# Routing from residual rows in two halves of tokens, gathering unnormalised rows, and a ninth weight slot

## The chip, the cores and the metric

The kernel runs on one core of one Trainium2 chip. The metric is the time of one execution in microseconds (us). The core's engines are TensorE (PE in the rows, its weight loads PEld), VectorE (DVE), ScalarE (ACT), GpSimd (POOL) and SyncE (SP, here the queue that issues nearly all DMAs). SBUF holds 128 partitions; PSUM has eight banks of 128 x 512 float32.

## The reference

One layer on 512 tokens of width 1024, all in float32: a mixer, then a mixture of experts (MoE), then a gated embedding, each added to the residual. What matters here is the second part:

```python
u = rms_norm(h, norm_ffn_g)                 # h * rsqrt(mean(h*h) + eps) * g
group_logits = u @ w_rg + b_rg              # 4 groups: the best one
exp_logits   = u @ w_re + b_re              # 8 experts a group: the best two of that group
gates = p_group * softmax(top_v)
for each expert e, each token that chose it:
    y = (silu(x @ w_gate_e[e]) * (x @ w_up_e[e])) @ w_down_e[e]     # 1024 -> 512 -> 1024
h = h + sum over the two choices of gate * y
```

There are 32 experts with three matrices of 2 MB each, 96 matrices or 201 MB in all. A token's two experts are computed and no others, but every expert's weights are read.

## The kernel before

**Stages.** The mixer is 15 blocks of four tiles: each tile is a product of float32 numbers that were split into a rounded high half (fp32r) and the rest, so a product takes three passes of 128 x 512. The last two blocks are `out`: tile c of them writes half of the residual of token block c % 4 (`residual`, lines 969 to 974), so that the four token blocks of 128 tokens (`h1` in `r1`) are complete one after the other, after tiles 4, 5, 6 and 7.

**Routing.** When a token block's residual is complete, ScalarE takes the sum of squares and the root (`norm`), VectorE multiplies by the root and the gain (`normalise`, line 859) and writes `u2` in an order of columns that lets TensorE read it in contiguous pieces. TensorE transposes `u2` (`transpose_rows`, line 1194), ScalarE copies the transposes to `u2T`, and `logits` makes the 36 logits of three token blocks at once and of the last block alone, transposed, with the router's weights as the stationary operand. `logits_by_token` turns them back and adds the two halves. VectorE then runs a chain of some twenty small operations on all four token blocks (`first_max` and what stands around it, lines 1036 to 1051), TensorE counts places (`before`, `ones`), and VectorE makes `pick`, a matrix of zeros and ones that says which token stands in which of the 64 places of each of two experts. `gather` multiplies the halves of `u2` (`u2_high`, `u2_low`) by `pick`: 8 products of 128 x 512 for each half of the columns. ScalarE copies the rows to `xrow`, TensorE transposes them (`transpose_x`, line 1331) and ScalarE copies the result to `xT`.

**Expert loop.** For each expert: `gate_and_up` (32 matmuls in two column tiles of 64), one half of the `gather` for the next pair of experts, `gather_info` (token numbers and gates, 8 small matmuls), `down` of the expert before (8 matmuls), on odd experts `transpose_x` for the next pair, and two transposes of the hidden rows. A float32 matmul shows as two records, so 32 of them are 64 rows in the trace. VectorE scales the result and GpSimd scatters it to DRAM by an indirect DMA. The order within the loop is written by hand, and is the same on each engine's queue at every run.

**Weights.** The 96 matrices go through the eight 2 MB slots of `ring` in a fixed order (`loads`): gate, up of expert 0 and 1, down of 0, then gate, up of e and down of e - 1. Eight of them are loaded ahead of the loop: two at the end of block 12, two after the first `out` block, four after the last (line 449; the last of these waits for the logits as well, whose transposes lie in slot 7). In the loop SP issues matrix n when matrix n - 8 has been read.

**Tail.** After the loop the two results of each token are read back (`y_back`), added to `h1` (line 1129), normalised, transposed and multiplied by the gate matrix (`ple_gate`), while TensorE also computes the embedding product (`ple`).

Of the kernel before, what the change touches and what calls it, by code (L numbers as in the profile page):

```python
# [15 lines left out]
ALU = mybir.AluOpType  # L16
# [15 lines left out]
SLOT = 4096  # L32
C = 64
# [3 lines left out]
def build(nc, x, p, norm_mix_g, w_in, conv_w, conv_b, w_rg, b_rg, w_ig, b_ig, lru_lambda, w_pool, pool_scale,  # L37
# [17 lines left out]
    assert NE % 4 == 0 and (3 * NE) % SLOTS == 0 and S == 512 and D == 1024  # L55
# [34 lines left out]
    with ctx:  # L90
# [27 lines left out]
        u2 = r2[:, :].rearrange("p (i d) -> p i d", i=TT)  # L118
        merged = r3[:, :].rearrange("p (k t) -> p k t", k=KD)
        u2T = ring[:, 7, :].rearrange("p (k t) -> p k t", k=KD)  # L120
# [46 lines left out]
        lgT = r4[:, 0:S]  # L167
        logit_parts = (slice(0, (TT - 1) * P), slice((TT - 1) * P, S))

# [3 lines left out]
        u2_low = r2_r[:, :].rearrange("p (i d) -> p i d", i=TT)  # L173
        u2_high = r3_r[:, :].rearrange("p (i d) -> p i d", i=TT)
        pick = sb("pick", [P, TT, 2, C], F32R)
# [4 lines left out]
        vecs = sb("vecs", [P, P])  # L180
# [20 lines left out]
        add_halves = sb("add_halves", [P, NL])  # L201
        g4 = sb("g4", [P, 4, TT, NG])
        t4 = sb("t4", [P, 12, TT])
        el = sb("el", [P, TT, NE])
        cand = sb("cand", [P, TT, NE])
# [18 lines left out]
        slot_full = [sem(f"slot_full{s}") for s in range(SLOTS)]  # L224
# [48 lines left out]
        lgT_psum = sem("lgT_psum")  # L273
        lgT_cleared = sem("lgT_cleared")
        lgT_ready = sem("lgT_ready")
        lgT_ready2 = sem("lgT_ready2")
# [9 lines left out]
        u2_high_ready = sem("u2_high_ready")  # L286
        u2_low_ready = sem("u2_low_ready")
# [19 lines left out]
        row_free = sem("row_free")  # L307
        y_in = [[sem(f"y_in{k}_{i}") for i in range(TT)] for k in range(2)]
# [18 lines left out]
        def slots_at(m):  # L327

            return 16 * (m // SLOTS + 1)


# [25 lines left out]
        def split_u2(eng, api, i):  # L357

            eng.wait_ge(u2_high_ready, i + 1)
            eng.wait_ge(ut_psum, 2 * (TT + i) + 2)  # L360
            api.tensor_tensor(u2_low[:, i, :], u2[:, i, :], u2_high[:, i, :], ALU.subtract).then_inc(u2_low_ready, 1)
# [6 lines left out]
        def wslot(n, k):  # L368
            return ring[:, n % SLOTS, :].rearrange("p (k f) -> p k f", k=k)


        T_PLE = 0
        T_PG = T_PLE + 1
        s0 = T_PLE % SLOTS
        wple = ring[:, s0, 0:KP * D].rearrange("p (k n) -> p k n", k=KP)
        p_rows = ring[:, s0, KP * D:KP * D + TT * KP * P].rearrange("p (i n) -> p i n", i=TT)
        pT = ring[:, s0, KP * D + TT * KP * P:KP * D + 2 * TT * KP * P].rearrange("p (k t) -> p k t", k=KP)
        y_back = ring[:, 5:7, :].rearrange("p s (i k d) -> p (s i) k d", i=2, k=2)
        ple = ring[:, 7, :].rearrange("p (i d) -> p i d", i=TT)
        u3 = u2  # L380
        u3T_high = slot_r[0][:, :].rearrange("p (k t) -> p k t", k=KD)
        u3T_low = merged_low
# [7 lines left out]
        def gate_part(kind, h):  # L390
            of = {"whole": ring[:, T_PG + h, :], "low": slot_r[T_PG + h][:, :], "high": slot_r[T_PG + 2 + h][:, :]}[kind]
            return of.rearrange("p (k f) -> p k f", k=KD)
# [5 lines left out]
        def _(sp):  # L398
# [6 lines left out]
            def small_loads():  # L405
# [13 lines left out]
                sp.dma_start(wrt[:, :, 0:NG], w_router_group[0].rearrange("(p k) n -> p k n", p=P)).then_inc(lru_in, 16)  # L419
                sp.dma_start(wrt[:, :, NG:NL], w_router_expert[0].rearrange("(p k) n -> p k n", p=P)).then_inc(lru_in, 16)  # L420
# [18 lines left out]
            def load_expert(n):  # L439

                which, e = loads[n % (3 * NE)]
                dst = ring[:, n % SLOTS, :]
# [8 lines left out]
            for m, n in ((0, FIRST_OUT), (6, FIRST_OUT), (3, FIRST_OUT + 1), (4, FIRST_OUT + 1),  # L451
                         (1, FIRST_OUT + 2), (2, FIRST_OUT + 2), (5, FIRST_OUT + 2), (7, FIRST_OUT + 2)):
                sp.wait_ge(tile_done, 4 * n)
                if m == 7:
                    sp.wait_ge(logits_psum, 1)
# [141 lines left out]
        def _(act):  # L597
# [148 lines left out]
            for i in range(TT - 1):  # L746
                u2_round(i)
# [731 lines left out]
```

## Time and profile before

| | |
|---|---|
| median of 3 runs | 918.71 us (914.36, 918.71, 919.59) |
| profiled execution | 918.7 us, its span 917.0 us |
| mean granted TensorE clock | 0.982 |
| busy: PE, PEld, DVE, ACT, POOL | 875.6, 583.8, 360.8, 260.5, 105.5 us |
| HBM read and written | 247.93 MB and 10.49 MB |

The span has four stretches: the mixer to about 352 us, routing and the first gather to 381 us, the expert loop to 842 us, and the tail to 917 us. A row of the chain of waits gives a start, a length, and what was being waited for or done; a row of the timeline gives start, busy time, engine, line, operation, output and inputs, and at its end the idle time before it with what ended it. The 1.7 us between the span and the time lie outside the instructions.

### The profile page before, as it was taken

The page shows a single profiled execution, that of the slowest core. Times are in us where ns is not written, and L with a number is a line of the kernel's source. Part 1 is how long each engine was busy: PE and PEld are TensorE (multiplying, and loading weights), DVE is VectorE, ACT ScalarE, POOL GpSimd, SP SyncE. Part 2 cuts the span into 40 slices and gives each one's busy share as a digit, 9 for nine tenths or more (in the row PEclk, how much of TensorE's full clock was granted, in tenths as well). Part 3 has the DMA queues.
Part 4 walks back from the last instruction along what each step waited for, and adds up shares of the span by engine and source line. Part 5 has one row for each costly group of instructions (what it writes and reads, how often), then busy time and mean ns, then how long its engine had stood idle before and what let it go on. Part 6 is the DMA issues. An engine that isn't in the chain of part 4 may idle for free.

```text
span 917.0 us, 12501 instructions
## 1 busy us (share of the span) xinstructions
PE 875.6 (95%) x5343; PEld 583.8 (64%) x5343; DVE 360.8 (39%) x544; ACT 260.5 (28%) x371; POOL 105.5 (12%) x82
## 2 busy tenths in 40 slices
PE   4999899999999997799999999999999999999896
PEld 3778687778888885555555555555555555554575
DVE  6599419952751635321121111211112111122865
ACT  7565326633232225110111001110101101011657
POOL 3429470000000001000000000000000000000000
PEclk8999999999999999799999999999999999999998
DMA  9222222211524665399999999999999999998802
GB/s 259 82 93 92 91 92 92 91 46 47 184 92 184 233 249 240 150 403 424 428 427 427 426 429 424 426 427 426 430 425 427 426 427 427 424 427 335 299 1 92
DMA packets 43295, 255.03 MB, mean 278 GB/s; under 512 B 8594, under 2 KB 9686, under 8 KB 30952
## 3 DMA queue, kind: packets, MB, share of 16 engines
q1 hardware_dynamic: 40248, 248.46, 66.8%
q0 software_dynamic: 2560, 4.20, 1.2%
q10 hardware_dynamic: 432, 1.57, 0.4%
q8 instruction: 42, 0.69, 0.3%
q14 instruction: 13, 0.11, 0.0%
HBM read 247.93 MB, written 10.49 MB: 282 GB/s over the span
## 4 chain that ended last, share of the span: by engine, by line
PE 81%; DVE 8%; DMA 6%; ACT 3%; issue 1%; SPq 0%; DVEq 0%; POOLq 0%; ACTq 0%
PE bank L1180 78%; DMA ring<-in_w_down_e_dram 4%; PE bank L1331 2%; DVE ring L922 1%; DVE ring L926 1%; PE bank L1365 1%; PE bank L1194 1%; DVE r L928 1%; DMA ring<-expert_rows 1%; DVE r L859 1%; DMA r<-in_x_dram 1%; DMA expert_rows<-r,row_i 1%; ACT junk L610 0%; DVE ring_rounded L343 0%; ACT ring_rounded L338 0%
## 5 line engine op out<-in xcount | busy, mean ns | idle before, releaser
L1180 PE MATMUL bank<-ring_rounded,ring_rounded 128*128 128x512 f32 x704 | 246.2, 393 | 1.7 <-ACT ring L798 1.7
L1180 PE MATMUL bank<-ring,junk 128*64 128x256 f32 x2048 | 240.5, 391 | 1.1 <-issue 0.6
L1180 PE MATMUL bank<-r_rounded,ring_rounded 128*128 128x512 f32 x704 | 231.8, 400 | 4.8 <-DVE ring_rounded L343 2.8
L1180 PEld LDWEIGHTS bank<-ring,junk 128*64 128x64 f32 x2048 | 141.4, 135 | 88.2 <-issue 4.8
L1180 PEld LDWEIGHTS bank<-r_rounded,ring_rounded 128*128 128x128 f32 x704 | 133.8, 190 | 36.9 <-DVE ring_rounded L343 3.6
L1180 PEld LDWEIGHTS bank<-ring_rounded,ring_rounded 128*128 128x128 f32 x704 | 132.9, 189 | 31.9 <-issue 2.4
L1180 PE MATMUL bank<-ring,hT 128*64 128x512 f32 x512 | 116.6, 597 | 0.7 <-DMA ring<-in_w_down_e_dram 0.7
L1103 DVE TENSOR_TENSOR sig<-sig,bank 128x256 f32<-128x256 f32 x32 | 13.5, 422 | 221.3 <-ACT sig L782 221.3
L782 ACT ACTIVATE sig<-bank 128x256 f32<-128x256 f32 x32 | 12.3, 385 | 297.7 <-PE bank L1180 297.7
L586 POOL DMA_INDIRECT expert_rows<-r,row_i x32 | 31.4, 981 | 448.3 <-DVE r L1085 448.3
L1180 PE MATMUL bank<-r_rounded,pick 128*128 128x512 f32 x272 | 72.9, 412 | 1.6 <-DVE pick L1030 1.6
L1180 PEld LDWEIGHTS bank<-ring,hT 128*64 128x64 f32 x512 | 34.2, 137 | 61.2 <-issue 59.9
L1085 DVE TENSOR_SCALAR r<-bank,gate_c 128x512 f32<-128x512 f32 x32 | 24.0, 751 | 117.3 <-PE bank L1180 117.3
L338 ACT ACTIVATE ring_rounded<-ring 128x2048 fp32r<-128x2048 f32 x28 | 53.6, 1913 | 43.1 <-DMA ring<-in_w_in_dram 18.5
L343 DVE TENSOR_TENSOR ring_rounded<-ring,ring_rounded 128x2048 fp32r<-128x2048 f32 x19 | 43.5, 2288 | 54.6 <-ACT ring_rounded L338 54.6
L1180 PEld LDWEIGHTS bank<-r_rounded,pick 128*128 128x128 f32 x272 | 49.7, 192 | 23.9 <-issue 14.6
L1180 PE MATMUL bank<-ring_rounded,r_rounded 128*128 128x512 f32 x128 | 49.9, 389 | 0.0
L343 POOL TENSOR_TENSOR ring_rounded<-ring,ring_rounded 128x2048 fp32r<-128x2048 f32 x9 | 42.4, 4727 | 63.6 <-ACT ring_rounded L338 63.6
L762 ACT ACTIVATE gain<-bank 128x512 f32<-128x512 f32 x34 | 20.3, 597 | 59.2 <-PE bank L1180 59.2
L766 ACT ACTIVATE junk<-bank 128x512 f32<-128x512 f32 x34 | 18.6, 595 | 58.2 <-PE bank L1331 58.2
L908 DVE SCALAR_TENSOR_TENSOR ring<-bank,prm,ring 128x511 f32<-128x511 f32 (+2 forms) x24 | 17.9, 747 | 37.1 <-ACT ring L646 36.5
L1180 PEld LDWEIGHTS bank<-ring_rounded,r_rounded 128*128 128x128 f32 x128 | 24.0, 188 | 4.9
(186 smaller groups left out, 650.5 us busy)
## 6 DMA issues: line engine op xcount, KB each, us to landing
ring<-in_w_gate_e_dram SPq DMA_DIRECT2D x32, 2048.0 KB
ring<-in_w_up_e_dram SPq DMA_DIRECT2D x32, 2048.0 KB
ring<-in_w_down_e_dram SPq DMA_DIRECT2D x32, 2048.0 KB
ring<-in_w_in_dram SPq DMA_DIRECT2D x18, 1024.0 KB, 7.2
r<-in_x_dram SPq DMA_DIRECT2D x8, 512.0 KB, 8.1
ring<-in_w_up_a_dram SPq DMA_DIRECT2D x4, 1024.0 KB, 6.2
ring<-in_w_out_dram SPq DMA_DIRECT2D x4, 1024.0 KB, 6.3
ring<-in_w_ple_gate_dram SPq DMA_DIRECT2D x4, 1024.0 KB, 14.0
```

The lines of the kernel that those rows point to most:

```text
L338: nc.scalar.activation(high_half(n, h), whole_half(n, h), ACT.Copy).then_inc(high_ready, 1)
L343: api.tensor_tensor(low_half(n, h), whole_half(n, h), high_half(n, h), ALU.subtract).then_inc(low_ready[low_engine[n, h]], 1)
L586: nc.gpsimd.indirect_dma_start(out=y_halves, out_offset=bass.IndirectOffsetOnAxis(ap=row_i[:, e:e + 1], axis=0), in_=yrow[:, e % 4, :], in ...
L762: nc.scalar.activation(xrow[:, h * HALF:(h + 1) * HALF], bank[6 + h][:, :], ACT.Copy).then_inc(xrow_ready, 1)
L766: nc.scalar.activation(xT[:, 4 * h:4 * h + 4, :, :].rearrange("p k e c -> p k (e c)"), bank[6 + h][:, :].rearrange("p (k n) -> p k n", k=4 ...
L782: nc.scalar.activation(sig[:, :], bank[2 + e % 2][:, 0:FE // 2], ACT.Sigmoid).then_inc(sig_ready, 1)
L859: v.scalar_tensor_tensor(out=dst, in0=src, scalar=rstd[:, q:q + 1], in1=view(gain[:, :]), op0=ALU.mult, op1=ALU.mult).then_inc(norm_done, 1)
L908: ins = v.scalar_tensor_tensor(out=y[:, d:S], in0=z[:, 0:S - d], scalar=tap(3 - d, c), in1=y[:, d:S], op0=ALU.mult, op1=ALU.add)
L1085: v.tensor_scalar(yrow[:, e % 4, :], bank[5][:, :], gate_c[:, e:e + 1], None, ALU.mult).then_inc(y_stored, 1)
L1103: v.tensor_tensor(sig[:, :], sig[:, :], gate_up[:, 0:FE // 2], ALU.mult).then_inc(gated, 1)
L1180: return nc.tensor.matmul(*a, **k)
L1331: ins = nc.tensor.transpose(bank[6 + h][:, k * P:(k + 1) * P], xrow[:, (4 * h + k) * P:(4 * h + k + 1) * P], ident[:, :])
```

## The change

**Routing.** No normalised rows are made. TensorE transposes the residual rows themselves (`transpose_h1`, with the stationary operand read at every 8th column), in the middle of the next `out` tile; the gain is multiplied into the router's weights once (`wrt`), and the root into the logits (`rstd` as the scalar of the first routing operation). The logits are made one token block at a time, tokens on partitions, with 36 moving columns (`logits`). Routing, places and `pick` are made for token blocks 0 and 1 first (`route(0)`, `find_places(0)`), then for 2 and 3; the first half stands ahead of the last `residual` on VectorE's queue. GpSimd has no part in it any more.

**Gather.** `gather` reads exact halves of the residual, `rows_high` in `r2` and `rows_low` in slot 6's place, each half of the output taking 4 of every 8 columns. The root of each gathered row comes by a small product of its own, `gather_scale` (pick times `rstd`, one moving column, four matmuls for each pair of experts); VectorE copies it (`copy_scale`) and ScalarE applies it in `copy_rows`. The gain is applied when the transposes are copied to `xT`, which moves from ScalarE to VectorE. `transpose_x` reads every 4th column of `xrow`.

**Weights.** Nine slots: the first three early, the other six after the last `out` tile, in an order of places `expert_slots` that takes in `r3` and `r1`. `r1` held the residual, so `h1` is restored after the loop from its halves, four additions on VectorE ahead of `gate_low`.

**Loop order.** `gather_info(e)` is made in expert e's own turn, `down` is cut in two with the second `transpose_x` between the parts, and `pick` has two buffers.

```diff
+            def transpose_h1(i):
+                pe.wait_ge(h1_ready, TT + i + 1)
+                for h in range(2):
+                    q = 2 * i + h
+                    if q >= 3:
+                        pe.wait_ge(rows_ready, q - 2)
+                    for k in range(4):
+                        ins = nc.tensor.transpose(bank[4 + q % 3][:, k * P:(k + 1) * P],
+                                                  h1[:, i, :].rearrange("p (q k) -> p k q", k=KD)[:, 4 * h + k, :], ident[:, :])
+                    ins.then_inc(rows_psum, 1)
+            def logits(i):
...
+                for k in range(KD):
+                    ins = mm(bank[7 if i < 2 else 0][:, i * 64:i * 64 + NL], h1T[:, k, i * P:(i + 1) * P], wrt[:, k, :],
+                             start=(k == 0), stop=(k == KD - 1))
+            def gather_scale(pair):
+                for i in range(TT):
+                    ins = mm(bank[0][:, 0:1], picked(pair)[:, i, :].bitcast(F32), rstd[:, TT + i:TT + i + 1], start=(i == 0),
+                             stop=(i == TT - 1))
+                ins.then_inc(scale_psum, 1)
...
+            for n in range(LEAD):
+                sp.wait_ge(tile_done, 4 * (FIRST_OUT + (n + 1) // 2 if n < 3 else len(blocks)))
+                if n == 7:
+                    sp.wait_ge(logits_psum, TT)
+                if n == 8:
+                    sp.wait_ge(rows_low_ready, TT)
+                    sp.wait_ge(row_std_done, TT)
+                load_expert(n)
...
                 for e in range(NE):
-                    gate_and_up(n0, e)
-                    pe.wait_ge(pick_ready, r * PAIRS + (e // 2 + 2))
-                    gather(e % 2)
+                    gate_and_up(r, n0, e)
+                    pe.wait_ge(pick_ready, r * PAIRS + (e // 2 + 3))
                     if e % 2 == 0:
-                        pe.wait_ge(info_ready, n0 * 2 + 2 * (e + 2))
-                        gather_info((e + 2) % NE)
-                    if e >= 1:
-                        down(n0, e - 1)
+                        pe.wait_ge(scale_ready, r * PAIRS + (e // 2 + 1))
+                        gather_scale(e // 2 + 1)
+                    gather(e // 2 + 1, e % 2)
                     if e % 2 == 1:
                         transpose_x(n0 + (e + 1), 0)
+                    gather_info(e)
+                    if e >= 1:
+                        down(r, n0, e - 1, (0, 1))
+                    if e % 2 == 1:
                         transpose_x(n0 + (e + 1), 1)
+                    if e >= 1:
+                        down(r, n0, e - 1, (2, 3))
                     transpose_hidden(n0, e)
...
+            for i in range(TT):
+                v.tensor_tensor(h1[:, i, :], rows_high[:, i, :], rows_low[:, i, :], ALU.add).then_inc(h1_restored, 1)
```

Where the instructions stand now. TensorE before, from the end of the last `out` tile on (`ident` with `r` is a transpose of `u2`, `wrt` with `ring` the transposed logits, `add_halves` the logits by token):

```order
L1180 MATMUL bank<-ring_rounded_51,ring_rounded_54 128x512 x4
L1194 MATMUL bank<-ident,r 128x128 x8
L1180 MATMUL bank<-ring,wrt 36x384 x8
L1194 MATMUL bank<-ident,r 128x128 x8
L1180 MATMUL bank<-add_halves,r 128x36 x3
L1180 MATMUL bank<-ring,wrt 36x128 x8
L1180 MATMUL bank<-add_halves,r 128x36
L1180 MATMUL bank<-routed_bf,before 128x32 x2
```

The same place now (`wrt,ring` are the logits by token, of token blocks 2 and 3; `pick` begins the gather of token blocks 0 and 1):

```order
L1210 MATMUL bank<-ring_rounded_51,ring_rounded_54 128x512 x4
L1210 MATMUL bank<-routed_bf,before 128x32 x2
L1210 MATMUL bank<-routed_bf,ones 128x32
L1264 MATMUL bank<-ident,r 128x128 x8
L1210 MATMUL bank<-wrt,ring 128x36 x16
L1210 MATMUL bank<-r_rounded_58,pick 128x512
L1210 MATMUL bank<-ring_rounded_55,pick 128x512
```

The two passes over the logits have become products with 36 moving columns and a 128-column stationary operand, and half of the routing's results are there before them.

TensorE now, at the end of `out` tile 6 and the beginning of tile 7; before, nothing but transposes stood between two tiles:

```order
L1210 MATMUL bank<-ring_rounded_51,ring_rounded_54 128x512 x4
L1210 MATMUL bank<-wrt,ring 128x36 x8
L1210 MATMUL bank<-ring_rounded_50,ring_rounded_54 128x512
L1210 MATMUL bank<-ring_rounded_50,r_rounded_59 128x512
L1210 MATMUL bank<-ring_rounded_50,ring_rounded_54 128x512
```

Eight logits matmuls of token block 1 now stand ahead of the last tile, as those of block 0 stand ahead of the one before it.

TensorE in the loop before, an even expert, from the end of `gate_and_up` to the first rows of the gather:

```order
L1180 MATMUL bank<-ring,junk 64x256 x24
L1383 ISA
L1180 MATMUL bank<-r_rounded_59,pick 128x512
L1180 MATMUL bank<-r_rounded_58,pick 128x512
L1180 MATMUL bank<-r_rounded_59,pick 128x512
```

And now:

```order
L1210 MATMUL bank<-ring,junk 64x256 x24
L1442 ISA
L1444 REGISTER_ALU
L1210 MATMUL bank<-rstd,pick 128x1 x4
L1210 MATMUL bank<-r_rounded_58,pick 128x512
L1210 MATMUL bank<-ring_rounded_55,pick 128x512
```

Four float32 matmuls with `pick` as a 128-column stationary operand and one moving column have come in, once for each pair of experts; everything else of the loop has the counts that it had.

## Rows read from the trace of the kernel before

**Rows 1.** TensorE's waits for weights, 400 to 860 us: total, times, longest

```profile
PE bank L1180 <- DMA ring<-in_w_down_e_dram: 0.7, 1, 0.7
PE bank L1180 <- DMA ring<-in_w_up_e_dram: 0.5, 1, 0.5
```

**Rows 2.** Busy time by stretch: us, PE, PEld, DVE, ACT, POOL (instructions), clock, DMA share, GB/s

```profile
360.70:361.50 0.80, 0.80 (x9) 0.79 (x7) 0.80 (x1) 0.80 (x2) 0.00 (x0) 1.00 1.05 451
```

**Rows 3.** The same view of longer stretches of routing and loop

```profile
364.00:370.00 6.00, 0.00 (x0) 0.00 (x0) 5.35 (x20) 0.44 (x1) 1.06 (x1) 0.63 1.01 429
...
381.40:388.90 7.50, 7.46 (x52) 4.72 (x54) 0.33 (x1) 0.04 (x1) 0.00 (x0) 0.77 0.18 37
```

**Rows 4.** Chain of waits, 320 to 917 us: start, length, what

```profile
352.39 0.70 DVE r L974
...
369.85 0.30 DVE routed_bf L1048
...
381.44 11.68 PE bank L1180 x88
...
478.87 0.37 PE bank L1365 x2
...
507.45 0.37 PE bank L1365 x2
...
842.22 0.76 DVE r L1085
```

**Rows 5.** Timeline of TensorE in the loop, expert 1's end and expert 2

```profile
400.82 2.11 PE L1180 MATMUL bank<-r_rounded,pick 128*128 128x512 f32 x8
402.86 3.65 PE L1180 MATMUL bank<-ring,hT 128*64 128x512 f32 x16
406.44 1.09 PE L1331 MATMUL bank<-ident,gain 128*128 128x128 f32 x8
407.37 0.38 PE L1365 MATMUL bank<-ident,hid 128*128 128x128 f32 x2
...
415.55 2.11 PE L1180 MATMUL bank<-r_rounded,pick 128*128 128x512 f32 x8
417.59 0.63 PE L1180 MATMUL bank<-info,pick 128*64 128x2 f32 x16
418.07 3.63 PE L1180 MATMUL bank<-ring,hT 128*64 128x512 f32 x16
```

**Rows 6.** Weight loads of the logits by token, on TensorE's load side

```profile
360.74 0.75 PEld L1180 LDWEIGHTS bank<-add_halves,r 128*128 128x128 f32 x6
```

**Rows 7.** Timeline of routing and first gather, 345 to 383 us

```profile
364.07 0.17 DVE L1019 TENSOR_REDUCE t<-lg 128x4 f32<-128x16 f32 x1
...
366.28 0.29 DVE L1019 TENSOR_REDUCE t<-el 128x4 f32<-128x128 f32 x1
366.60 0.29 DVE L1020 TENSOR_TENSOR cand<-el,t 128x128 f32<-128x128 f32 x1
...
371.50 0.69 DVE L1030 TENSOR_TENSOR pick<-iota,place 128x512 fp32r<-128x512 f32 x1
...
372.34 5.53 PE L1180 MATMUL bank<-r_rounded,pick 128*128 128x512 f32 x16 [1.58 <-DVE pick L1030]
```

**Rows 8.** SP's queue: start, length, issues of expert weights

```profile
363.79 0.33 SPq L449 DMA_DIRECT2D ring<-in_w_down_e_dram  x1
...
386.92 0.33 SPq L449 DMA_DIRECT2D ring<-in_w_gate_e_dram  x1
...
797.43 3.95 SPq L449 DMA_DIRECT2D ring<-in_w_down_e_dram  x2
```

**Rows 9.** Timeline at the loop's end and in the tail

```profile
833.02 3.65 PE L1180 MATMUL bank<-ring,hT 128*64 128x512 f32 x16 [0.70 <-DMA ring<-in_w_down_e_dram]
...
847.93 2.29 DVE L354 TENSOR_TENSOR ring_rounded<-ring,ring_rounded 128x2048 fp32r<-128x2048 f32 x1 [3.99 <-ACT ring_rounded L793]
...
852.69 1.22 DVE L1129 TENSOR_TENSOR r<-r,ring 128x1024 f32<-128x1024 f32 x1
```

More of the change, by code:

```diff
@@ L32 @@
 SLOT = 4096
+LEAD = 9
 C = 64
@@ L439, in load_expert @@
             def load_expert(n):
-                which, e = loads[n % (3 * NE)]
-                dst = ring[:, n % SLOTS, :]
+                which, e = loads[n]
                 if which < 2:
@@ new lines, in find_places @@
+            def find_places(half):
+                at = slice(2 * half, 2 * half + 2)
+                dve.wait_ge(places_psum, half + 1)
+                dve.wait_ge(routed_ready, 2 * half + 2)
+                after(v.scalar_tensor_tensor(out=cand[:, at, :],
+                                             in0=bank[1 + half][:, 0:2 * NE].rearrange("p (i e) -> p i e", i=2),
+                                             scalar=1.0, in1=routed[:, at, :], op0=ALU.add, op1=ALU.mult))
+                after(v.tensor_scalar(place[:, 0:NE, at].rearrange("p e i -> p i e"), cand[:, at, :], -1.0, None, ALU.add))
+                make_pick(0, at)
@@ new lines, in make_pick, with copy_scale @@
+            def make_pick(pair, at=slice(0, TT)):
+                n = at.stop - at.start
+                where = place[:, 2 * pair:2 * pair + 2, at].rearrange("p e i -> p i e")
+                v.tensor_tensor(pick[:, pair % 2, at, :, :], iota[:, :].unsqueeze(1).unsqueeze(1).to_broadcast([P, n, 2, C]),
+                                where.unsqueeze(3).to_broadcast([P, n, 2, C]), ALU.is_equal).then_inc(pick_ready, 1)
+            def copy_scale(at):
+                dve.wait_ge(scale_psum, at)
+                v.tensor_copy(row_scale[:, :], bank[0][:, 0:1]).then_inc(scale_ready, 1)
@@ L1051, in _ @@
-            after(v.tensor_tensor(routed[:, :, :], oh1[:, :, :], oh2[:, :, :], ALU.add))
-            dve.wait_ge(places_psum, 1)
-            after(v.scalar_tensor_tensor(out=cand[:, :, :], in0=bank[5][:, 0:TT * NE].rearrange("p (i e) -> p i e", i=TT),
-                                         scalar=1.0, in1=routed[:, :, :], op0=ALU.add, op1=ALU.mult))
-            after(v.tensor_scalar(place[:, 0:NE, :].rearrange("p e i -> p i e"), cand[:, :, :], -1.0, None, ALU.add))
-            make_pick(0)
+                    if c > TT:
+                        row_rstd(c - TT - 1)
+                        if c < 2 * TT - 1:
+                            rows_split(dve, c - TT - 1)
@@ L1059, in _ @@
+            find_places(1)
+            rows_split(dve, TT - 1)
+            copy_scale(1)
+            after(v.tensor_reduce(t4[:, 0, 0:1], bank[2][:, 2 * NE:3 * NE], AX.X, ALU.max))
+            v.tensor_scalar(rounds_i[:, :], t4[:, 0, 0:1], 1.0 / C, 0.5 - 0.5 / C, ALU.mult, ALU.add).then_inc(rounds_ready, 1)
             dve.wait_ge(gexp_ready, 1)
@@ L1072, in _ @@
                                    op0=ALU.mult, op1=ALU.add).then_inc(info_made, 1)
-            after(v.tensor_reduce(t4[:, 0, 0:1], bank[5][:, TT * NE:(TT + 1) * NE], AX.X, ALU.max))
-            v.tensor_scalar(rounds_i[:, :], t4[:, 0, 0:1], 1.0 / C, 0.5 - 0.5 / C, ALU.mult, ALU.add).then_inc(rounds_ready, 1)
+            copy_xT(0, 0)
+            copy_xT(0, 1)
+            make_pick(1)
             def take_info(e, at):
@@ L1248, in _ @@
                                     pe.wait_ge(*lows_at(n, g))
+                            if kind == "out" and c > TT and (part, k) == ("high", 4):
+                                transpose_h1(c - TT - 1)
                             if (kind, c, part) == ("out", 0, "high"):
```

457 lines of the change are left out of this document (229 added, 228 removed).

## Prediction

> **What bounds the kernel now.** I read the chain of waits first. It is TensorE from beginning to end, but with three kinds of stretch around the place that changes. At 352.39 us the last `out` tile is done; at 381.44 the expert loop begins; at 842.22 VectorE takes the loop's last result [rows 4]. So routing with its first gather lasts 29.05 us, and the loop 460.8. In routing the path goes through small steps of VectorE and copies: between 364 and 370 us TensorE does nothing and VectorE is busy for 5.35 of 6 us [rows 3].
>
> Then the loop. A pair of experts takes 507.45 - 478.87 = 28.58 us on the chain [rows 4], and the timeline shows where it goes: a gather of 8 takes 2.04 us (400.82 to 402.86), a `down` 3.58, eight transposes 0.93 (406.44 to 407.37), a `gather_info` 0.48 (417.59 to 418.07), the rest `gate_and_up` and the hidden rows' transposes, with no gap [rows 5]. So TensorE's own queue is the bound of the loop. Last I looked at whether the weights are near to being it too. They are: TensorE waits for weights for 0.7 + 0.5 = 1.2 us in the whole loop [rows 1], at its end, for the matrix that SP issued at 797.43 (the last but one of the 96) and that lets `down` start at 833.02 [rows 8, 9]. The first matrix of the loop was issued at 386.92 [rows 8]. From there to 833.02 lie 87 matrices, 5.13 us each. TensorE uses one in 28.58 / 6 = 4.76 us. The eight matrices loaded ahead make up for the difference, and are just used up at the end. The loop has two bounds that lie about a microsecond apart, which decides much below.
>
> **Ahead of the loop.** Take T as the end of the last `out` tile, now 352.4.
>
> T itself moves. Logits of token blocks 0 and 1 are now made between the last three tiles: 8 float32 matmuls each, 16 records, each with a 128-column load. The nearest row is the logits by token, the only float32 loads of 128 columns with few moving columns: six loads in 0.75 us, of which the last takes 0.19, so (0.75 - 0.19) / 5 = 0.112 us from one to the next [rows 6], at full clock [rows 2]. That is 16 x 0.11 = 1.8 us a block, 3.5 for two. The transposes of token block 2, which stood behind the last tile, now stand inside it: 0.9 [rows 5]. T becomes 356.8. ScalarE and VectorE are no cover lost here: their work for a block ends before TensorE needs it.
>
> From T on, the path is: residual 0.7 [rows 4]; eight transposes 0.9; the copy of their second half 0.7 (on VectorE, as long as the residual, which also reads a bank); logits of block 3, 1.8, but behind those of block 2, so that they end at T + 5.3. VectorE by then has done `find_places(0)` and the third `rows_split`. `route(1)` is 21 operations: 8 on at most 72 numbers a partition at 0.2 us each (0.17 for 16 numbers, and a gap of 0.03), and 13 on 64 numbers. One on 128 numbers takes 0.32 from start to start (366.28 to 366.60) [rows 7]; by the line between 16 and 128, one on 64 takes 0.255. Sum 1.6 + 3.3 = 4.9, so T + 10.4. Places 0.5, the two operations of `find_places` and half a `pick` (0.69 for a whole one [rows 7], so 0.42 with its fixed part) 1.2: T + 12.1. `gather_scale` 0.9, six products of the gather at 0.255 [rows 5] 1.5, the last two 0.5: T + 15. Copy, transposes, copy 0.7 + 0.5 + 0.7 (each copy of a bank taken as the residual's 0.7): T + 16.9, or T + 17.2 since VectorE reaches `copy_xT` behind the gates' arithmetic. Half of the gather (8 products) is done before, in the shadow of `route(1)`.
>
> This is at full clock. Before, the clock was at 0.63 over 364 to 370 [rows 3], a mixture of the levels 1.2 and 2.4 GHz, after TensorE had stood idle, and 16 gather products took 5.53 us [rows 7] where the loop needs 4.1. TensorE now still idles for some 3 us within `route(1)`, so I add 0.8 (between 0 and 2.2): the loop begins at T + 18.0 = 374.8, 6.6 us earlier than before. So of 29 us 11 go, and 4.4 come back ahead of T.
>
> **The loop.** `gather_scale` is 4 float32 matmuls, 8 records with 128-column loads, once a pair. No row shows one moving column on 128 stationary ones. From below: `gather_info` has 16 records in 0.48 us, 0.03 each, but with 64-column loads in two column tiles side by side [rows 5]; that gives 0.24 us a pair, 3.8 in 16 pairs. From above: 8 x 0.112 [rows 6] and 0.1 for one more change of form, 1.0 a pair, 16 in all. I take 0.88 a pair, 14.1 in all, since the row on which the upper end rests has the same load and differs in 36 columns against 1, which do not bind there. Nothing hides it: TensorE's queue is the bound, and it is in order. The split of `down`, the place of `gather_info` and the second `pick` add no matmul; VectorE, which gets `copy_xT` (2 x 0.7 a pair) and the scale, has at least half a `down`, 1.8 us, between each copy and its use. SP gets no new wait. Nor do I count a gain from the clock, which stood at 0.77 in the first 7.5 us of the loop [rows 3]: up to 1.7 us, kept for the range.
>
> Without its 1.2 us of waits the old loop is 459.6 us. So it ends at 374.8 + 459.6 + 14.1 = 848.5.
>
> The weights no longer bind. Six matrices are issued from T on, the later ones before the queue runs dry, and matrix 9 when the first gate is read, at about 378.5, while the sixth of them lands at 388. So the stream has no hole, where before it had one (last issue at 363.79, next at 386.92 [rows 8]). The last but one lands at 356.8 + 92 x 5.13 = 829, the last at 834; TensorE wants them about 839 and 845. The ninth slot and the closed hole give some 10 us of slack, and buy 1.2.
>
> **The tail.** VectorE restores `h1` with four additions of 1.22 [rows 9], 4.9 us, between the copy of the embedding's transposes and `gate_low`. Before, it had finished with `gate_low` (2 x 2.29) and stood idle until the first rows came back at 852.69, 10.5 after the loop's end [rows 9]. Now: scaling of the last result 0.8 [rows 4], the transposes' wait and copy about 1.0, then 4.9 + 4.6, together 11.3. So 0.8 late for the first addition, and the next waits for its own rows; I take 0.3 (0 to 0.8).
>
> **Sum.** 918.7 (the profiled execution; it equals the median) - 6.6 + 14.1 - 1.2 + 0.3 = 925.3. I say 925: slower by 0.7%. A measurement of this kernel tells a change from none at about 0.5%, 4.6 us.
>
> **Rivals.** First, the scale costs what `gather_info`'s records cost, or hides in the load side under the products beside it. For it: 0.03 us a record is seen in this very loop [rows 5]. Against it: those loads are half as wide and run in two column tiles. Then TensorE would end the loop at 838.2, and the last matrix at 834 plus the last `down` of 3.65 gives 837.7: both bounds at once, time 915, faster. More than this can't come out, since the weights need their 93 x 5.13 us from T on.
>
> Second, the stationary operand that is read with holes costs time. Transposes of residual rows take every 8th column, those of `xrow` every 4th. No row of before has such a load: all its stationary operands are contiguous. Bounds: nothing, or, if such a load takes twice the contiguous time, 0.11 more on each transpose [rows 6]: 8 a pair, 14 us in the loop and 2.6 ahead of T and behind it; time 942. Half of it gives 933. The Trainium skill, "SBUF — State Buffer", in its note on SBUF cachelines, speaks against the change here: accesses keep full bandwidth only when a 16-byte line is hit at least twice, and a stride of 4 float32 numbers hits each once. No trace here shows it. By the same rule the gather's new order (4 of 8 columns, whole lines) is free; were it not, at twice 0.255 a product, 65 us would come, and I give that 2 in 100.
>
> Third, the start gains nothing: the half routing or the last half of the gather runs at the low clock level throughout and the logits twice as long. Then the loop begins near 379, time 929; this lies in the range of the forecast.
>
> **How the numbers follow.** Forecast, the scale at about 0.11 a record and free strides: 55 in 100, 921 to 930. Cheap scale: 17 in 100, 912 to 919. Strided loads: 24 in 100, 929 to 942. The rest, 4, beyond. A change of sign needs the scale to cost under 0.45 a pair. Slower by over 0.5% (above 923.3): 38 of the 55, all of 24 and 4, so 0.66. Within: 17 of the 55 and 5 of the 17, 0.22. Faster: 0.12. Range 915 to 939.
>
> **What the profile would show.** Right: records of `rstd,pick` x8 that push the first gather row 0.9 us back in every even expert; a pair of about 29.5 us; loop begin near 375; no wait of TensorE for weights; DMA share below 1 in the loop's middle. Wrong: a pair of 28.8 with waits for weights at the end (first rival); transposes with `gain` at over 1.2 us for eight (second); a loop that begins after 379 (third). An unchanged pair and a begin near 375 would break the argument altogether.

## The result, and the profile after

The changed kernel takes 932.31 us (median of 4 runs, 931.2 to 933.0) against 918.56: ratio 1.0157, with a 95% interval of 1.0124 to 1.0191. It is slower by 13.8 us where 6.3 were forecast. The sign is right, and the loss is 2.2 times the forecast one. The profiled execution is 931.2 us with a span of 929.5 (before 918.7 and 917.0); the rows below are of these two executions, which lie 12.5 us apart.

The chain of waits of the changed kernel, with the rows that answer to [rows 4] (start, length, what):

```profile
355.25 0.70 DVE r L968
...
365.64 0.24 DVE routed_bf L1004
...
367.40 5.08 PE bank L1210 x15
...
375.05 10.98 PE bank L1210 x96
```

The last `out` tile ends at 355.25 (352.39 before), the loop begins at 375.05 (381.44). Its end, from the same view:

```profile
848.40 1.89 PE bank L1210 x8
850.30 0.03 issue
850.32 0.39 DVE r L1111
850.72 0.27 issue
850.99 0.42 DVE hT L1115
851.41 0.14 issue
851.55 3.67 PE bank L1210 x16
855.22 0.03 issue
855.24 0.76 DVE r L1111
```

The loop's last `down` ends at 855.22 (842.19 before), so the loop lasts 480.2 us against 460.8, and the tail 74.3 against 74.8. The start is 6.4 us earlier, the loop 19.4 us longer and the tail 0.5 shorter: that is the whole difference of 12.5 us.

The timeline of TensorE in one pair of experts of the changed kernel (start, busy, engine, line, operation; `128*128` or `128*64` is the tile of an instruction, as the profile names it; most rows of the gather are left out), which answers to [rows 5]:

```profile
408.91 1.05 PE L1210 MATMUL bank<-rstd,pick 128*128 128x1 f32 x8
409.82 0.48 PE L1210 MATMUL bank<-r_rounded,pick 128*128 128x512 f32 x1
...
411.85 0.63 PE L1210 MATMUL bank<-info,pick 128*64 128x2 f32 x16
412.33 3.63 PE L1210 MATMUL bank<-ring,hT 128*64 128x512 f32 x16
415.90 0.44 PE L1407 MATMUL bank<-ident,hid 128*128 128x128 f32 x2
...
425.39 0.40 PE L1210 MATMUL bank<-ring_rounded,pick 128*128 128x512 f32 x1
425.63 0.64 PE L1366 MATMUL bank<-ident,gain 128*128 128x128 f32 x4
426.19 0.63 PE L1210 MATMUL bank<-info,pick 128*64 128x2 f32 x16
426.68 1.92 PE L1210 MATMUL bank<-ring,hT 128*64 128x512 f32 x8
428.53 0.75 PE L1366 MATMUL bank<-ident,gain 128*128 128x128 f32 x4
429.21 1.94 PE L1210 MATMUL bank<-ring,hT 128*64 128x512 f32 x8
431.07 0.44 PE L1407 MATMUL bank<-ident,hid 128*128 128x128 f32 x2
```

Read from start to start: `gather_scale` takes 0.91 us (408.91 to 409.82). The eight transposes, in two groups, take 0.56 + 0.68 = 1.24, where the one group of before took 0.93. The two halves of `down` take 1.85 + 1.86 = 3.71 against 3.58. A pair takes 29.94 us (mean of nine between 470 and 640 us, from one transpose of the hidden rows to the next but one), against 28.58. TensorE has no wait for weights any more; the view of its waits from 400 to 860 us shows only the loop's end and the tail:

```profile
PE bank L1210 <- DVE hT L1115: 0.9, 1, 0.9
PE bank L1210 <- DVE ring L1149: 0.9, 1, 0.9
```

Busy time by stretch around the loop's beginning (columns as in [rows 2]):

```profile
366.00:369.00 3.00, 1.97 (x19) 1.86 (x19) 2.17 (x6) 0.31 (x2) 0.00 (x0) 0.62 0.98 421
369.00:372.50 3.50, 3.50 (x10) 2.58 (x9) 2.36 (x12) 0.00 (x0) 0.00 (x0) 0.50 1.04 445
372.50:375.00 2.50, 1.71 (x9) 1.14 (x8) 0.88 (x2) 2.42 (x3) 0.00 (x0) 0.79 0.99 423
375.00:382.50 7.50, 7.45 (x65) 4.67 (x65) 1.01 (x2) 0.12 (x1) 0.00 (x0) 1.00 1.01 428
```

The granted clock is 0.50 during the last part of the gather, the low level; TensorE had idled 3.3 us in `route(1)` before it. It is 1.00, the full level, in the first expert, where before it stood at 0.77 [rows 3].

### The profile page after: what moved, and what is told of

Read it like the earlier page. It is cut to its first block, busy times and chain, and to the rows that moved or that the text cites. A ratio compares the mean times of both kernels' runs of the same rounds, so it can differ in the third digit from the quotient of the medians.

```text
span 929.5 us, 12845 instructions
## 1 busy us (share of the span) xinstructions
PE 896.1 (96%) x5471; PEld 604.6 (65%) x5471; DVE 381.6 (41%) x617; ACT 243.5 (26%) x334; POOL 102.9 (11%) x80
## 4 chain that ended last, share of the span: by engine, by line
PE 86%; DVE 8%; ACT 3%; DMA 2%; issue 1%; DVEq 0%; SPq 0%; POOLq 0%; ACTq 0%
PE bank L1210 81%; PE bank L1366 2%; DVE ring L916 1%; PE bank L1407 1%; DVE ring L920 1%; DVE r L922 1%; ACT ring_rounded L345 1%; DVE ring_rounded L350 1%; DMA r<-in_x_dram 1%; DMA ring<-in_w_up_b_dram 1%; PE bank L1223 1%; DMA ring<-expert_rows 0%; DVE r L854 0%; PE bank L1264 0%; DVE ring L921 0%
## 5 line engine op out<-in xcount | busy, mean ns | idle before, releaser
L1210 PEld LDWEIGHTS bank<-ring_rounded,ring_rounded 128*128 128x128 f32 x768 | 144.6, 189 | 34.3 <-issue 2.4
L1210 PE MATMUL bank<-ring,junk 128*64 128x256 f32 x1408 | 166.1, 389 | 0.4 <-DVE junk L1030 0.4
L1210 PEld LDWEIGHTS bank<-ring,junk 128*64 128x64 f32 x1408 | 96.6, 134 | 61.4 <-issue 3.5
L1210 PE MATMUL bank<-r,junk 128*64 128x256 f32 x640 | 76.4, 389 | 0.0
L1210 PEld LDWEIGHTS bank<-r,junk 128*64 128x64 f32 x640 | 43.5, 134 | 28.1 <-issue 1.7
L1210 PE MATMUL bank<-r_rounded,pick 128*128 128x512 f32 x136 | 57.6, 425 | 0.0
L1210 PE MATMUL bank<-ring_rounded,pick 128*128 128x512 f32 x136 | 54.3, 401 | 0.0
L1030 DVE TENSOR_TENSOR junk<-bank,gain_col 128x512 f32<-128x512 f32 x34 | 23.4, 691 | 52.6 <-PE bank L1366 52.6
L767 ACT ACTIVATE gain<-bank,row_scale 128x512 f32<-128x512 f32 x34 | 23.3, 687 | 73.4 <-PE bank L1210 73.4
L1210 PEld LDWEIGHTS bank<-r_rounded,pick 128*128 128x128 f32 x136 | 26.1, 192 | 11.2 <-issue 6.5
```

Source lines behind the costliest of these rows:

```text
L767: nc.scalar.activation(xrow[:, h * HALF:(h + 1) * HALF], bank[6 + h][:, :], ACT.Copy, scale=row_scale[:, 0:1]).then_inc(xrow_ready, 1)
L1030: v.tensor_tensor(xT[:, 4 * h:4 * h + 4, :, :].rearrange("p k e c -> p k (e c)"), bank[6 + h][:, :].rearrange("p (k n) -> p k n", k=4), bc ...
L1210: return nc.tensor.matmul(*a, **k)
```

## The experiments

They ran in three groups (e1 to e4; e5, g1, g2 and g4; e6, g5, g6 and b1), each group beside the kernel before on the same chip. "Pair" is the length of a pair of experts, measured as above.

| kernel | pair, us | time, us | ratio to before, interval |
|---|---|---|---|
| before | 28.58 | 918.6 | |
| changed | 29.94 | 932.3 | 1.0157 (1.0124 to 1.0191) |
| e1_whole_down | 29.88 | 933.9 | 1.0184 (1.0139 to 1.0228) |
| e2_packed_transposes | 29.81 | 930.7 | 1.0145 (1.0101 to 1.0189) |
| e3_no_scale_in_loop | 29.06 | 917.8 | 1.0009 (0.9986 to 1.0032) |
| e4_scale_in_tiles | 29.47 | 925.1 | 1.0092 (1.0067 to 1.0117) |
| e5_transposes_first | 29.88 | 930.7 | 1.0174 (1.0146 to 1.0201) |
| g1_scaled_rows | 29.02 | 915.8 | 0.9999 (0.9986 to 1.0012) |
| g2_filler | 29.02 | 915.1 | 0.9985 (0.9973 to 0.9998) |
| g4_eight_slots | 29.02 | 916.4 | 0.9993 (0.9977 to 1.0010) |
| e6_order_of_before | 29.64 | 928.7 | 1.0117 (1.0089 to 1.0145) |
| g5_scaled_order_of_before | 28.75 | 914.2 | 0.9964 (0.9945 to 0.9984) |
| g6_strided_moving | 31.77 | 961.7 | 1.0473 (1.0443 to 1.0503) |
| b1_cut_in_before | 28.89 | 917.9 | 1.0004 (0.9982 to 1.0025) |

The kernel before itself had medians of 915.7, 916.7 and 918.5 us beside the three groups, so ratios are compared and not times. The pair decides: the nine pairs of a profile differ by 0.03 us at most.

**e1_whole_down.** Gather, `gather_info`, then:

```diff
-                    if e % 2 == 1:
-                        transpose_x(n0 + (e + 1), 0)
...
-                        down(r, n0, e - 1, (0, 1))
+                        down(r, n0, e - 1, (0, 1, 2, 3))
                     if e % 2 == 1:
+                        transpose_x(n0 + (e + 1), 0)
                         transpose_x(n0 + (e + 1), 1)
-                    if e >= 1:
-                        down(r, n0, e - 1, (2, 3))
```

> The changed kernel with one edit: on odd experts `down` is whole again and both halves of transpose_x stand behind it, as before. Same matmuls, same strides. In the changed kernel a pair of experts takes 29.93 us on TensorE against 28.58; 0.91 of the difference is gather_scale, 0.44 is not. Theory A (the cut costs it: each return from transposes to `down` and back is a change of form): pair 29.5 us, loop 7 us shorter, time about 925.3. Theory B (the stationary operand read at every 4th column costs it): pair stays 29.9, time about 932.

The pair hardly moved. The timeline of this kernel shows why (some rows of other engines left out):

```profile
485.85 0.39 PE L1210 MATMUL bank<-ring_rounded,pick 128*128 128x512 f32 x1
486.18 0.63 PE L1210 MATMUL bank<-info,pick 128*64 128x2 f32 x16
486.66 3.63 PE L1210 MATMUL bank<-ring,hT 128*64 128x512 f32 x16
490.23 1.23 PE L1366 MATMUL bank<-ident,gain 128*128 128x128 f32 x8
491.01 0.69 DVE L1030 TENSOR_TENSOR junk<-bank,gain_col 128x512 f32<-128x512 f32 x1 [5.27 <-PE bank L1366]
491.29 0.38 PE L1407 MATMUL bank<-ident,hid 128*128 128x128 f32 x2
491.85 3.85 PE L1210 MATMUL bank<-ring,junk 128*64 128x256 f32 x32 [0.18 <-DVE junk L1030]
```

`down` is back at 3.57 and the transposes at 1.06, 0.32 less together. But the last product of the gather now takes 0.33 us until `gather_info` begins, where it took 0.24 until the first transpose (425.39 to 425.63 in the changed kernel), and the next gate matmul waits 0.18 us for the copy `copy_xT`, which the change gave to VectorE with the gain in it. The cut was the cover of that copy. The pair is 0.06 shorter with a new wait of 0.18 in it, so on TensorE itself the cut costs 0.24 here. The kernel lost with one hand most of what it won with the other, and at the loop's end it waits 2.0 us for `hT` where the changed kernel waits 0.9.

**e2_packed_transposes.**

```diff
-                                              xrow[:, h * HALF:(h + 1) * HALF].rearrange("p (q j) -> p j q", j=4)[:, k, :],
+                                              xrow[:, (4 * h + k) * P:(4 * h + k + 1) * P],
```

> The changed kernel, but transpose_x reads contiguous columns of xrow in place of every 4th; the rows of xT then are in another order than the weights' rows, so the experts' results are not the reference's, at the same amount of work. Theory A (the cut costs): pair stays 29.9, time about 932. Theory B (strided stationary operand): the two groups of four transposes shrink from 0.56 + 0.68 to about 0.93 together, pair about 29.6 or less, time about 926.

The two groups take 0.53 + 0.59 = 1.12 in place of 1.24, and the pair is 0.12 shorter: 2 us in 16 pairs. So the stride is real and small, 0.015 us a transpose where the rival's upper bound had 0.11. Theory B had expected 0.3.

**e3_no_scale_in_loop.** `gather_scale` and `copy_scale` are out of the loop body.

> The changed kernel without gather_scale and its copy inside the loop: the scale of the first pair of experts stays in use for all, so that part of the computation is left out. If TensorE's queue is the loop's bound and the weights have slack: pair 29.0 us, loop 14.6 us shorter, time about 917.7, no wait for weights. If the load side hides part of the 8 records, or the weights take over as the bound, less: over 920.

Pair 29.06, so the scale costs 0.88, exactly the forecast's term; the time is 917.8 beside 915.7 for the kernel before in that group. 0.48 us a pair remain unexplained by the scale.

**e4_scale_in_tiles.**

```diff
-                    ins = mm(bank[0][:, 0:1], picked(pair)[:, i, :].bitcast(F32), rstd[:, TT + i:TT + i + 1], start=(i == 0),
-                             stop=(i == TT - 1))
+                    for h in range(2):
+                        ins = mm(bank[0][h * C:(h + 1) * C, 0:1], pick[:, pair % 2, i, h, :].bitcast(F32),
+                                 rstd[:, TT + i:TT + i + 1], start=(i == 0), stop=(i == TT - 1))
```

> The changed kernel with gather_scale in two column tiles: 8 matmuls (16 records) with 64-column loads in place of 4 (8 records) with 128-column loads, same result. If the load of the stationary operand sets the record's time, and two column tiles run side by side as in gather_info: 16 x 0.03 = 0.5 us in place of 0.91, pair 29.5, time about 925.5. If each record costs a fixed 0.11 whatever its width: 1.8 us, pair 30.8, time about 946.

```profile
497.70 0.58 PE L1210 MATMUL bank<-rstd,pick 128*64 128x1 f32 x16
```

Twice the records in half the time (497.70 to 498.21, 0.51), pair 29.47. A record takes 0.03 us in place of 0.11, so its price is not a fixed one. The run halves the width of the load and puts two column tiles side by side at once: sixteen loads of half the width one after another would take 0.91 us again if the width alone set their time (an estimate from the 0.91 measured), so the width alone does not explain it. How much is due to either of the two, the run doesn't tell.

**e5_transposes_first.** As e1, with both `transpose_x` between `gather_info` and the whole `down`.

> The changed kernel with `down` whole and both halves of transpose_x ahead of it, behind gather_info; same matmuls and strides. e1_whole_down got back 0.31 us a pair on TensorE but then waited 0.2 for VectorE's copies of the transposes. Theory A (the cut costs about 0.3 a pair, by its two extra changes between transposes and `down`, and it was there to cover VectorE's copies): no wait, pair 29.6 us, time about 927. Theory C (the cut costs nothing; `down` and the transposes are slow for another reason): pair 29.9, time about 932.

No wait in the loop but the 0.9 us for `hT` at its end, and yet 29.88: the 29.6 that I gave for theory A was wrong. The transposes took 1.16 us behind `gather_info`, with `down` after them, where in e1 they took 1.06 with the hidden rows' transposes after them, and `gather_info` took 0.56 in place of 0.49. The timelines give the reason if one counts not the pieces but the changes between `128*128` and `128*64` from one instruction to the next. `gate_and_up`, `gather_info` and `down` are `128*64`; the gather, the scale and all transposes are `128*128`. So counted, this order has ten changes a pair, as many as the changed kernel; e1 has eight, as the kernel before. Whole `down` or not, the number of these changes had not gone down.

**e6_order_of_before.** As e1, with `gather_info` of odd experts behind the hidden rows' transposes (but for the last expert).

> The changed kernel with the loop's order of before on odd experts: `down` whole, both halves of transpose_x, the hidden rows' transposes, and then gather_info (for the last expert it stays ahead of `down`). e1 had the same without gather_info behind, and waited 0.2 us a pair for VectorE's copies. Theory A (each change between forms on TensorE costs 0.1 to 0.2 us, and this order has the fewest, and hides the copies behind gather_info): pair 29.94 - 0.32 = 29.6 us, no wait, time about 927. Theory C (the order doesn't matter, e1 and e5 at 29.88 show it): pair 29.9, time about 931.

Pair 29.64, as theory A said, with eight changes: the cut's 0.3 is back, and no wait for the copies is left, since `gather_info` stands between them and the gate matmuls, as in the kernel before. The time of 928.7 is above the 927 expected; the loop's end again has the 2.0 us wait for `hT` that e1 has.

**b1_cut_in_before.** The converse, in the kernel before:

```diff
-                        down(n0, e - 1)
...
                         transpose_x(n0 + (e + 1), 0)
+                        down(n0, e - 1, (0, 1))
                         transpose_x(n0 + (e + 1), 1)
+                        down(n0, e - 1, (2, 3))
```

> The kernel before with one part of the change: on odd experts the transposes and `down` stand as transpose, half of `down`, transpose, other half; the copies stay on ScalarE. Theory A (the cut itself costs about 0.3 us a pair on TensorE): pair 28.9, loop 5 us longer less up to 1.2 of waits for weights, time about 922. Theory C: pair 28.6, time about 918.

Pair 28.89, 0.31 more, with contiguous transposes and ten changes in place of eight. What such a change looks like, with the rows of the weight loads (PEld):

```profile
488.68 0.59 PEld L1331 LDWEIGHTS bank<-ident,gain 128*128 128x128 f32 x4
488.91 0.60 PE L1331 MATMUL bank<-ident,gain 128*128 128x128 f32 x4
489.44 0.20 PEld L1180 LDWEIGHTS bank<-ring,hT 128*64 128x64 f32 x4 [0.17 <-issue]
489.44 1.94 PE L1180 MATMUL bank<-ring,hT 128*64 128x512 f32 x8
491.30 0.42 PEld L1331 LDWEIGHTS bank<-ident,gain 128*128 128x128 f32 x4 [0.81 <-issue]
491.31 0.66 PE L1331 MATMUL bank<-ident,gain 128*128 128x128 f32 x4
```

From the gather to the transposes, both `128*128`, the first load starts 0.23 us before its matmul, while the last product still runs. At the two changes after it the load starts no more than 0.01 us ahead of the matmul; nothing of it is hidden.

The loop of its profile is 3.8 us longer than before's, but the ratio of times is 1.0004: of a loss of some 4 us the runs show none outside their interval of 0.2%. The pair confirms the price of the cut; the time alone would not.

**g1_scaled_rows.** e5's order, and the root put on when the rows are split:

```diff
-                nc.scalar.activation(rows_high[:, i, :], h1[:, i, :], ACT.Copy).then_inc(rows_high_ready, 1)
+                act.wait_ge(rstd_ready, i + 1)
+                nc.scalar.activation(rows_high[:, i, :], h1[:, i, :], ACT.Copy,
+                                     scale=rstd[:, TT + i:TT + i + 1]).then_inc(rows_high_ready, 1)
...
+                    after(v.scalar_tensor_tensor(out=h1[:, i, :], in0=h1[:, i, :], scalar=std[:, TT + i:TT + i + 1],
+                                                 in1=y_back(i, k), op0=ALU.mult, op1=ALU.add))
```

> e5's order, and no gather_scale at all: the rows are multiplied by the root when they are split (ScalarE's copy takes rstd as its scale, VectorE's subtraction becomes a multiply and subtract of the same length), and in the tail std multiplies them back within the first addition. Same result up to rounding. Theory: pair 28.7 us, TensorE by itself ends the loop about 836, and the last matrix lands about 832 to 834 with its `down` of 3.6 behind it, so both bounds meet: time 912 to 914, faster than before. Rival (multiplying adds to the path of routing or the tail): over 916.

Pair 29.02, and TensorE waits for no weights: the loop ends at 839.6. The 28.7 and the 912 to 914 us that I expected did not come: they took it that e5's order was free of the cut's price, and it wasn't. The pair is e5's less 0.86, so the whole scale is gone, and the tail of 74.3 us is as long as the changed kernel's; the order's ten changes are still in.

**g2_filler.**

```diff
+            for _ in range(12):
+                mm(bank[3][:, :], picked(0)[:, 0, :], rows_high[:, 0, 0:HALF], start=True, stop=True)
             places(1)
```

> g1_scaled_rows with 12 useless products of 128 x 512 into a free bank on TensorE while VectorE does route(1), so that TensorE's clock doesn't fall there. Theory A (the low clock costs the last gather part 1.5 to 2.4 us, but the weights end the loop): the loop begins about 2 us earlier, TensorE waits about as much more for weights at the end, time within 1 us of g1. Theory B (TensorE is still the only bound): time 2 us below g1. Theory C (the clock doesn't follow the filler): nothing changes, loop begin as in g1.

Theory C, nearly: the loop begins at 374.11 in both. The filler cut TensorE's idle time in `route(1)` from 2.2 to 0.6 us, and over 363 to 366 us the granted clock was 1.00 against 0.51 in g1. But over 369 to 372 it was 0.63 against 0.56: the fall came later and still within the gather. The gather's last part was 0.3 us shorter (2.66 against 2.96) and the transposes behind it 0.3 longer (1.12 against 0.81).

**g4_eight_slots.**

```diff
+                    sp.wait_ge(gate_psum, 1)
...
-                    wait_expert_read(n - LEAD)
+                    wait_expert_read(n - LEAD + 1)
```

> g1_scaled_rows, but matrix 8 is only issued when the first gate has been read, and matrix n when matrix n - 8 has: the ninth place is there and never full, as with eight slots. Theory A (the gain of the weights' side is the closed hole behind the last `out` tile, not the ninth slot): the stream still has no hole, since matrices 3 to 7 keep it busy until about 381 us and matrix 8 is issued about 379: time within 1 us of g1. Theory B (the ninth slot carries it): one matrix less ahead, up to 5 us later.

Same pair, no wait for weights, and a time within 0.6 us of g1 (the loop of its profile begins 0.6 later). The ninth slot is worth nothing that shows here; with eight the stream has no hole either (DMA share 1.01 over 365 to 390 us in both). This was tried at a pair of 29.02 only, not at g5's 28.75.

**g5_scaled_order_of_before.** g1's rows with e6's order.

> g1_scaled_rows with the loop's order of e6. Theory A: pair 28.7 us (before's 28.58 and 0.12 for the strided transposes), loop 5 us shorter than in g1, time 911 to 913 with the weights' stream close behind or binding (waits of up to 2 us for weights at the end). Theory C: pair 29.0, time 916 as g1.

Pair 28.75, time 914.2, a little above the 911 to 913 expected. It is faster than the kernel before by 0.4% (interval 0.2 to 0.5%), and, by the two ratios, than the changed one by 1.9%. The pair is g1's less 0.27, for two changes fewer. Its longest wait of TensorE in the loop:

```profile
PE bank L1205 <- DVE hT L1109: 2.0, 1, 2.0
```

TensorE waits 2 us once, at the loop's end, for VectorE, and not for weights. So my estimate that the weights would bind at about this point was too early.

**g6_strided_moving.** g5, and the stride on the other operand:

```diff
-                          part[:, i, :].rearrange("p (q h j) -> p h q j", h=2, j=4)[:, h, :, :], **flags)
+                          part[:, i, :].rearrange("p (q h j) -> p h j q", h=2, j=4)[:, h, :, :], **flags)
...
-                                              xrow[:, h * HALF:(h + 1) * HALF].rearrange("p (q j) -> p j q", j=4)[:, k, :],
+                                              xrow[:, (4 * h + k) * P:(4 * h + k + 1) * P],
```

> g5 with the stride moved from the transposes' stationary operand to the gather's moving one: the gather reads every 8th column of the halves (fp32r, 32 bytes apart), and transpose_x reads contiguous columns; same result. Theory D (strided reads cost as little on the moving side as e2 showed on the stationary one, 0.12 us a pair there): pair 28.6 to 28.7, time as g5. Theory E (a moving operand that takes one number from each line of SBUF can't keep up at one column a cycle): gather 3 to 4 us in place of 2, pair 31 to 33, time over 945.

Theory E, in kind. The costliest groups (line, engine, operation, count, busy us, mean ns) of the changed kernel, and under it those of g6:

```profile
L1210 PE MATMUL bank<-r_rounded,pick 128*128 128x512 f32 x136 | 57.6, 425 | 0.0
L1210 PE MATMUL bank<-ring_rounded,pick 128*128 128x512 f32 x136 | 54.3, 401 | 0.0
```

```profile
L1205 PE MATMUL bank<-r_rounded,pick 128*128 128x512 f32 x136 | 84.9, 626 | 1.0 <-DVE pick L1020 1.0
L1205 PE MATMUL bank<-ring_rounded,pick 128*128 128x512 f32 x136 | 82.5, 608 | 0.0
```

55.5 us more in 34 gathers of eight products, 1.6 each; the transposes are contiguous again and take 0.93, as in the kernel before. The change's own pattern, 4 of 8 columns, costs nothing: its gather takes 2.03 us (409.82 to 411.85) as before's took 2.04.

## Why the prediction was wrong

**The step that failed** is "The split of `down`, the place of `gather_info` and the second `pick` add no matmul". That was true, and I took it to mean that they cost nothing; the term was put at zero without a reason. In a loop where TensorE's queue is the bound, the count of matmuls isn't its length: each change between `128*128` and `128*64` instructions costs too. The new order has ten of them a pair in place of eight and costs about 0.3 us a pair: 0.31 in the kernel before (b1), 0.30 in the changed one (against e6), 0.27 in the scaled one (g1 against g5), 0.24 in e1. That is 0.12 to 0.16 a change, and 5 us in the loop. The prediction itself had allowed 0.1 "for one more change of form" in the upper bound of the scale, and none for the cut. The runs show the price, and the rows show that the first load is not hidden at such a change; that this is all of the price was not tested. The transposes' stride, which I had put into a rival and at nothing in the sum, is 0.12 a pair (e2), 2 us. Together 0.42 of the 0.48 that e3 leaves; 0.06 stays unassigned. With 16 x 0.48 = 7.7 us the forecast of 925 would have been 933.

**The scale** was right: 0.88 a pair forecast, 0.88 by e3. That a record with one moving column takes as long as one with 36 was the reason given, and holds: 0.114 us (0.91 / 8) against 0.109 for the 32 records of the logits behind the last tile.

**The start** came out right in this profile, and partly by luck. The last tile's end moved by 2.9 us, forecast 4.4; but in e1 to e6, with the same start, it lay between 355.3 and 356.9, and in the two kernels with before's start at 352.4 and 351.6, so the step is between 3 and 5 and the forecast is not refuted. Over the changed kernel and e1 to e6 the loop began at 375.1 to 376.8, 375.8 on average, 5.4 us before the 381.2 of the kernel before and b1; the 6.4 of the one profile flatters the 6.6 forecast. From there to the loop it took 19.8 us, forecast 18.0: up to `pick` the sum fits (T + 12.1), its parts to about 0.3 us, and then the low clock makes the scale 1.7 us in place of 0.9, and the gather's last 8 products 0.42 each in place of 0.23. I had allowed 0.8 for it, and it took 2.3.

**Small terms.** The 1.2 us of waits for weights went, as forecast. The first expert got 1.6 us back from the clock: 12.05 us before (381.44 to 393.49), and 10.44 now without its scale (375.05 to 386.40, less 0.91); I had kept that for the range. The loop's end lost 0.65: before, `gather_info` stood between the hidden rows' transposes and the last `down` while VectorE copied `hT`; now VectorE scales a result first, and TensorE waits for `hT`. Sum of the loop: 14.1 + 7.7 - 1.2 - 1.6 + 0.65 = 19.65, measured 19.4. The tail is 0.5 shorter, forecast 0.3 longer. The restored `h1` is no cost that shows in its length, though in g1 and g5 the four additions, 4.54 us together, stand in the chain of waits.

**The weights' slack** was right in its sign, and the ninth slot by itself buys nothing (g4). That the changed kernel is slower isn't the weights' doing in any part: TensorE never waits for them. One sign of being right was itself wrong, a DMA share below 1 in the loop's middle: it is 1.01 from 420 to 800 us. The prediction's own numbers forbade it, for a pair of 29.5 us uses a matrix every 4.92 us, still faster than the stream's 5.13.

**The rivals.** The cheap scale is refuted by e3. The strided load is true at a seventh of its upper price (0.015 against 0.11 us a transpose), and would not by itself have moved the time by more than a measurement can tell. Its sign, eight transposes at over 1.2 us, came true at 1.24, but with contiguous reads they still took 1.12 (e2): most of the excess over 0.93 is the cut's. "The start gains nothing" is false, its low clock true. The case that came, the scale and the cut together, I had not named.

## What to carry to other kernels

Where TensorE's own queue is the bound, price a reordering also by its changes between tile shapes (`128*128`, `128*64`) and not only by its instructions: count them in both orders, and measure from start to start across the changes that the trace of before already has. Put a factor that goes with a row onto the row when it is written anyhow (here at the split, at no cost), and not into a matmul of its own, whose record costs the same for one moving column as for 36. And before an order is undone, ask what stands behind the piece that was moved: the cut covered a copy, and taking it away alone gained next to nothing.

## What the runs showed of the hardware

**A change of tile shape.** Two more changes a pair between `128*128` and `128*64` instructions, with the same matmuls, cost 0.24 to 0.31 us in four comparisons (b1 against before, the changed kernel against e6, g1 against g5, e5 against e6), 0.12 to 0.16 each. Between instructions of one shape the next load starts up to 0.23 us ahead of its matmul, across a change not at all (b1's rows).

**Stride on the two operands of a matmul.** A stationary operand read at every 4th float32 costs 0.015 us a transpose (e2 against the changed kernel), and one at every 8th nothing that shows: eight such transposes of the residual took as long as before's of contiguous rows. The chain of the changed kernel, and of the kernel before under it:

```profile
343.39 0.88 PE bank L1264 x8
```

```profile
346.02 0.88 PE bank L1194 x8
```

A moving fp32r operand at every 8th number costs 1.6 us in eight products of 128 x 512, near a factor of 1.8 (3.6 against 2.03). The Trainium skill, "SBUF — State Buffer", in its note on SBUF cachelines, says that an access pattern needs two hits on a 16-byte line for full bandwidth. The gather agrees with it on both sides, whole lines at full rate and one hit a line at little over half. The stationary loads hardly show such a penalty, 0.015 us at every 4th number and none at every 8th; there the measurement decides. The same note gives four float32 numbers as the stride that is still free, which is near what e2 shows.

**A column of its own.** Eight float32 records with a 128-column load and one moving column take 0.91 us (changed kernel), sixteen with 64-column loads in two column tiles 0.51 (e4). The Trainium skill, "TensorE: Matmul & The Clock Gate", section on LDWEIGHTS, gives the time of a load by its columns alone, 128 / 1.2 = 107 ns; the trace's 0.11 a record agrees. By the same rule sixteen loads of 64 columns would take about 0.85 us one after another, an estimate, so the 0.51 of e4 is not explained by the width alone.
